# Three 1024x1024 products of a two-layer block, each formed as seven quarter products

## Chip, cores, metric

The kernel runs on one core of one Trainium2 chip. The metric is the device time of one execution in microseconds (us). The program is written out by hand, engine by engine, in one block: TensorE (PE) multiplies, VectorE (DVE) and ScalarE (ACT) move and combine tiles, GpSimd (POOL) helps and issues accumulating transfers, SyncE (SP) issues loads. The engines meet by semaphores only.

## What is computed

Two layers follow one another on x of 512 tokens by 1024 features, all in float32. The part that the change touches ends the mixer of the second layer:

```
mixed  = spatial gating of the first branch      (512 x 1024), in features-by-tokens as u_t
o      = forgetting attention, 16 heads           (512 x 1024), as att_t
merged = sigmoid(gate_b) * (o @ w_branch_b)  +  sigmoid(gate_a) * (mixed @ w_branch_a)
h      = h + merged @ w_out
h      = h + gated feed-forward of rmsnorm(h)     (phases up0, down0, ...)
```

The first layer, ahead of this, is a convolution with a chunked state scan (phases xbc, qk, z, v, wo_ssd, wo_att) and a feed-forward (ff1_g, ff2_g).

## The kernel before

**Precision.** Each float32 operand is split in a high part, rounded to the matmul's own format (ACT copies to `_hi`), and a low part, the rest (DVE subtracts, to `_lo`). A product is three passes: high by high, high by low, low by high (lines 767 to 769).

**Strips.** A weight matrix of 1024x1024 is read in 4 strips of 256 columns, 1 MB each, through three slots (`w_hi`, `w_lo`; the raw strip lies where the slot's low part goes). `strip_split` counts finished strips, `hi_split` high parts. SP loads strip s when the strip three before is used up (`unit_done`, two per strip: line 590). `PHASES` lists all phases with their strips; their order is the order of PE's work.

**A plain phase** (`stream`, `feature_k`) forms 8 output tiles of 128 features x 512 tokens, each over 8 k and 3 passes, in banks 0 to 3 of PSUM. DVE evacuates each tile.

**Seven products, as there is already.** ff2_0 to ff2_2, down0 and down1 take a product of two 2x2 block matrices as seven block products (`seven`, weights made by `A_PARTS`, data by `T_PARTS`). There the data is the stationary operand and 512 weight columns move. The sums of weight parts are formed in SBUF by accumulating transfers that POOL issues (`part_sums`, line 714), each waited for by the next.

**The stage that is changed.** During gate_a DVE evacuates gate tiles, and ACT and DVE split the attention's output (`split_attention`, into b_hi, b_lo). In branch_b DVE multiplies each result tile into `merged`, and low_a splits u_t (into a_hi, a_lo). In branch_a each tile is multiplied into gate_t, added to `merged`, and split into b. In out2 each tile is added to x (`add_x`), and the norm of the next phase (`high`, `square`, `low`, `add_square` under "ffn2") follows tile by tile. `direct_sums`, `direct_rms` form the root (rstd) while PE is in up0. The first evacuations of up0 (`up_pad`) need rstd; up0 uses banks 0 to 3.

**Work that lies early.** In xbc, ACT goes through tiles m: `first_tap(m)`, `silu(m - 1)`, `keep_xs(m - 4)` and every second time the high part of a strip; PE turns tiles with `turn_xs`, after `keep_xs` has freed its bank. Between qk and z, ACT issues on its own DMA queue `cum_kept<-cum` (line 1566), waits for it, and issues `seg_in<-cum_kept` (`load_cum`, line 1575). POOL masks what is loaded (line 647), ACT takes exponentials, DVE multiplies (line 2277), and PE's y matmuls (line 744) wait for that. After the last chunk ACT issues the load of `head_bias` (line 1600), which DVE's memset (line 2338) waits for and the first attention needs. POOL stages that attention's heads right after its share in z.

## Time and profile before

| | us |
|---|---|
| time, median of 3 runs | 1606.91 (1606.77 to 1607.81) |
| time of the profiled execution | 1607.59 |
| its span | 1605.9 |

Busy, of the span: PE 99%, weight loads (PEld) 81%, DVE 67%, ACT 44%, POOL 11%. The transfers move 195 MB at a mean of 122 GB/s, in three queues of weight: q1 (SP's), q0 (POOL's, accumulating), q10 (ACT's).

How to read it: matmuls are pipelined, so the duration of one is longer than its distance from the next; how many start in a stretch gives the pace. "Idle before, releaser" is the time for which an engine stood before an instruction, and what ended that. A row of a transfer issue shows the time that the issuing engine spent, not the transfer.

### The profile page before, as it was taken

To read this page: it belongs to the slowest core of one execution; us is meant where nothing else is said; L and a number is where in the kernel's file an instruction comes from. 1 tells how busy PE (TensorE), PEld (TensorE's weight loads), DVE (VectorE), ACT (ScalarE), POOL (GpSimd) and SP (SyncE) were. 2 spreads that over 40 slices of the span, in tenths; PEclk is the share of its full clock that TensorE was granted. 3 is DMA by queue.
4 is the path that set the end of the run, shared out by engine and by line. 5 is a ranking of instruction groups with operands and counts; after the bars stand their busy time and mean duration, and the time that the engine had idled before them with its cause. 6 is when DMAs were issued, how large, how long until landed. Compare 5 with 4: busy or idle time off the path is not lost.

```text
span 1605.9 us, 20446 instructions
## 1 busy us (share of the span) xinstructions
PE 1587.6 (99%) x8187; PEld 1305.8 (81%) x8187; DVE 1078.5 (67%) x1494; ACT 710.6 (44%) x1018; POOL 181.5 (11%) x263
## 2 busy tenths in 40 slices
PE   9999999999999999999999999999999999999998
PEld 7877777888888888878788887888888888888888
DVE  6756788669393865657744477445566876878857
ACT  6524575545252524415662156342334443443544
POOL 0001055000000000024500255000000000000000
PEclk9999999999999999999999999999999999999999
DMA  5233321264757522331022211322237347344221
GB/s 191 80 106 125 123 95 53 79 210 131 236 132 235 131 106 94 116 138 72 27 105 83 101 53 53 136 101 105 93 143 262 102 135 238 93 154 158 105 106 53
DMA packets 32894, 195.14 MB, mean 122 GB/s; under 512 B 4320, under 2 KB 6816, under 8 KB 11296
## 3 DMA queue, kind: packets, MB, share of 16 engines
q1 hardware_dynamic: 25056, 160.20, 27.0%
q0 software_dynamic: 2880, 20.97, 6.8%
q10 hardware_dynamic: 4864, 12.66, 2.2%
q8 instruction: 65, 1.06, 0.3%
q14 instruction: 29, 0.24, 0.0%
HBM read 187.50 MB, written 6.32 MB: 121 GB/s over the span
## 4 chain that ended last, share of the span: by engine, by line
PE 87%; DVE 7%; issue 2%; ACT 2%; POOL 1%; DMA 0%; DVEq 0%; ACTq 0%; POOLq 0%
PE bank L767 20%; PE bank L769 19%; PE bank L768 19%; PE bank L1189 3%; PE bank L1190 3%; PE bank L1191 3%; PE bank L815 3%; PE bank L817 3%; PE bank L816 3%; PE bank L1000 1%; PE bank L775 1%; PE bank L985 1%; DVE w_lo L2370 1%; PE bank L744 1%; DVE up_c L2668 1%
## 5 line engine op out<-in xcount | busy, mean ns | idle before, releaser
L767 PE MATMUL bank<-a_hi,w_hi 128*128 128x512 f32 x1160 | 456.8, 394 | 0.6 <-DVE x L2030 0.6
L769 PE MATMUL bank<-a_hi,w_lo 128*128 128x512 f32 x1160 | 452.0, 390 | 0.0
L768 PE MATMUL bank<-a_lo,w_hi 128*128 128x512 f32 x1160 | 451.6, 389 | 0.0
L1375 ACT ACTIVATE w_hi<-w_raw 128x2048 fp32r<-128x2048 f32 x95 | 181.3, 1908 | 184.5 <-DMA w_raw<-in_strips 182.7
L769 PEld LDWEIGHTS bank<-a_hi,w_lo 128*128 128x128 f32 x1160 | 217.8, 188 | 45.9
L767 PEld LDWEIGHTS bank<-a_hi,w_hi 128*128 128x128 f32 x1160 | 217.9, 188 | 45.3 <-issue 2.3
L768 PEld LDWEIGHTS bank<-a_lo,w_hi 128*128 128x128 f32 x1160 | 218.0, 188 | 43.0 <-issue 0.2
L1951 DVE TENSOR_TENSOR w_lo<-w_raw,w_hi 128x2048 fp32r<-128x2048 f32 x92 | 210.9, 2293 | 54.4 <-ACT w_hi L1375 54.3
L1189 PE MATMUL bank<-w_hi,t_hi 128*128 128x512 f32 x280 | 109.3, 390 | 0.1
L1191 PE MATMUL bank<-w_hi,t_lo 128*128 128x512 f32 x280 | 109.0, 389 | 0.0
L1190 PE MATMUL bank<-w_lo,t_hi 128*128 128x512 f32 x280 | 109.0, 389 | 0.0
L767 PE MATMUL bank<-b_hi,w_hi 128*128 128x512 f32 x240 | 93.6, 390 | 0.4 <-DVE b_lo L2684 0.4
L768 PE MATMUL bank<-b_lo,w_hi 128*128 128x512 f32 x240 | 93.4, 389 | 0.0
L769 PE MATMUL bank<-b_hi,w_lo 128*128 128x512 f32 x240 | 93.4, 389 | 0.0
L815 PE MATMUL bank<-w_hi,a_hi 128*128 128x512 f32 x224 | 90.8, 405 | 0.0
L714 POOL DMA_DIRECT2D a_part<-in_parts x20 | 17.4, 868 | 643.6 <-DMA a_part<-in_parts 431.9
L816 PE MATMUL bank<-w_lo,a_hi 128*128 128x512 f32 x224 | 87.4, 390 | 0.0
L817 PE MATMUL bank<-w_hi,a_lo 128*128 128x512 f32 x224 | 87.4, 390 | 0.0
L1845 ACT ACTIVATE up_c<-up_pad,conv_w 128x512 f32<-128x512 f32 x44 | 35.8, 816 | 115.1 <-DVE up_pad L2022 115.1
L2668 DVE SCALAR_TENSOR_TENSOR up_c<-up_pad,conv_w,up_c 128x512 f32<-128x512 f32 x88 | 65.8, 747 | 1.8 <-ACT up_c L1845 0.3
L2370 DVE TENSOR_TENSOR w_lo<-a_part,w_hi 128x2048 fp32r<-128x2048 f32 x25 | 57.1, 2285 | 10.7 <-ACT w_hi L1664 10.7
L2022 DVE TENSOR_TENSOR up_pad<-bank,rstd 128x512 f32<-128x512 f32 x44 | 30.3, 691 | 49.4 <-PE bank L769 49.4
(364 smaller groups left out, 2658.0 us busy)
## 6 DMA issues: line engine op xcount, KB each, us to landing
w_raw<-in_strips SPq DMA_DIRECT2D x107, 1024.0 KB, 4.8
a_part<-in_parts SPq DMA_DIRECT2D x25, 1024.0 KB, 7.4
a_part<-in_parts POOLq DMA_DIRECT2D x20, 1024.0 KB, 9.1
spare<-in_parts SPq DMA_DIRECT2D x5, 1024.0 KB, 15.0
spare<-in_strips SPq DMA_DIRECT2D x5, 1024.0 KB, 4.9
seg_in<-cum_kept ACTq DMA_DIRECT2D x16, 256.0 KB, 3.5
x_kept<-x ACTq DMA_DIRECT2D x2, 2048.0 KB, 9.2
x<-x_kept SPq DMA_DIRECT2D x2, 2048.0 KB, 9.9
```

The lines of the kernel that those rows point to most:

```text
L767: mm(ps[:, :], w_hi[slot][:, k, cols], hi[:, k, :], start=(k == 0), stop=False)
L768: mm(ps[:, :], w_hi[slot][:, k, cols], lo[:, k, :], start=False, stop=False)
L769: return mm(ps[:, :], w_lo[slot][:, k, cols], hi[:, k, :], start=False, stop=(k == kt - 1))
L815: mm(bank[j][:, :], hi[:, q, tok], w_hi4[slot][:, k, :], start=(q == 0), stop=False)
L816: mm(bank[j][:, :], hi[:, q, tok], w_lo4[slot][:, k, :], start=False, stop=False)
L817: return mm(bank[j][:, :], lo[:, q, tok], w_hi4[slot][:, k, :], start=False, stop=(q == KT - 1))
L1189: mm(ps[:, :], hi[:, k, tok], w_hi4[slot][:, k, :], start=(first and k == 0), stop=False)
L1190: mm(ps[:, :], hi[:, k, tok], w_lo4[slot][:, k, :], start=False, stop=False)
L1191: last = mm(ps[:, :], lo[:, k, tok], w_hi4[slot][:, k, :], start=False, stop=(end and k == W4 - 1))
L1375: run(w_hi[j], w_raw[j], ACT.Copy).then_inc(hi_split, 1)
L1951: v.tensor_tensor(w_lo[j], w_raw[j], w_hi[j].bitcast(F32), ALU.subtract).then_inc(strip_split, 1)
L2668: v.scalar_tensor_tensor(up_c[q], up_pad[q][:, j:j + T], flat[:, at * (CONV2 + 1) + j:at * (CONV2 + 1) + j + 1], up_c[q], ALU.mult, ALU.ad ...
```

## The change

The phases branch_b, branch_a and out2 get 7 strips each instead of 4: seven products of 512x512 weight parts by 4 k-tiles x 256 tokens. A quarter of the data is a half of the features (k-tiles) by a half of the tokens. The weights are the stationary operand as before, and 256 token columns move. Data sums (four per product) are made on POOL (`fold_sums`), all high parts on ACT and all low parts on DVE. Of the products' results, some are kept and combined on ACT and DVE (`keep_first`, `keep_second`, `keep_sums`, `take`), so that a result quarter is ready after products 3, 5, 6 and 7 (the first by take_first).

The four weight sums that are needed are formed in DRAM (tensor `pre`, 4 kinds x 3 matrices x 1 MB): ACT issues 12 copies DRAM to DRAM in xbc, POOL 6 accumulating transfers ahead of the first attention, 3 behind it and 3 behind the third ff2 phase. SP then loads the 21 strips through two buffers per product (`fold_raw`), in x's place for the first two products, and x itself comes back during out2's start. PE's order of phases and everything from up0 on stay; the strip counts shift by 9.

```diff
+FOLD = ["branch_b", "branch_a", "out2"]
+QUADS = [(0, 0), (1, 0), (0, 1), (1, 1)]
+FOLD_BANK = [4, 6, 4, 6, 2, 6, 2]
+FOLD_QUAD = [0, 1, 2, 0, 1, 3, 2]
+FOLD_SOURCE = [(0, 0), 0, (1, 0), 2, 1, 3, (1, 1)]
+PRE_SUMS = [(0, 1), (0, 0), (0, 0), (1, 0)]
+PHASES += [(name, 7) for name in FOLD]
...
 # SP
+                if s in FOLDED:
+                    n = s - FIRST[FOLD[0]]
+                    if n == 0:
+
+                        sp_eng.wait_ge(pv_done, 2 * 3 * HEADS8)
+                        sp_eng.wait_ge(summed, 16 * (12 + 4 * FF_SEVEN))
+                    elif n == 14:
+
+                        sp_eng.wait_ge(fold_step, FOLD_STEP0 + 5)
+                    elif n == 15:
+
+                        sp_eng.wait_ge(*low_ready(s - 3))
+                    elif n != 1:
+                        sp_eng.wait_ge(*low_ready(s - 2))
+                    f, i = FOLDED[s]
+                    source = FOLD_SOURCE[i]
+                    sp_eng.dma_start(flat(fold_at(s)), fold_part(f, source) if i in (0, 2, 6) else pre[source, f]).then_inc(fold_loaded[n % 3], 16)
+                    if n == 15:
+
+                        sp_eng.wait_ge(*low_ready(s - 2))
+                        sp_eng.dma_start(x, x_kept).then_inc(x_loaded[0], 16)
...
 # POOL
+            pool.wait_ge(copied, 16 * 12)
+            for kind, part in ((0, (1, 1)), (1, (0, 1))):
+                for f in range(3):
+                    pool.dma_start(pre[kind, f], fold_part(f, part), accum_op=ALU.add, max_dma_last_dim=8192).then_inc(summed, 16)
             pool.wait_ge(unit_done, 2 * FIRST["v"] + 2)
             clear_stage1(0)
             attention("1", "qk")
+            pool.wait_ge(summed, 16 * 6)
+            for f in range(3):
+                pool.dma_start(pre[2, f], pre[0, f], accum_op=ALU.add, max_dma_last_dim=8192).then_inc(summed, 16)
...
+            def fold_sums(f, n):
+
+                src, at = fold_src[f], FOLD_SUM0 + 4 * f
+                a11, a12, a21, a22 = (quad(src, *q) for q in ((0, 0), (0, 1), (1, 0), (1, 1)))
+                if n == 0:
+                    if f == 0:
+                        pool.wait_ge(att_out, 3 * HEADS8)
+                    elif f == 1:
+                        pool.wait_ge(a_ready, KT)
+                        pool.wait_ge(unit_done, 2 * FIRST["branch_b"])
+                    else:
+                        pool.wait_ge(merged_ready, 3)
+                    ins = pool.tensor_tensor(quad(fold_three[f], 1, 0), a11, a21, ALU.subtract)
...
 # PE
-            stream("branch_b", feature_k, B, ready=lambda k: pe.wait_ge(att_lo, 4 + k + 1))
-            stream("branch_a", feature_k, A, ready=wait_tiles(amix_lo))
-            stream("out2", feature_k, B, ready=wait_tiles(m_lo))
...
+            def folded(f):
+
+                for i in range(7):
+                    s = FIRST[FOLD[f]] + i
+                    slot, (t, k0) = s % W_SLOTS, QUADS[FOLD_QUAD[i]]
+                    hi, lo = quad(fold_hi[f], t, k0), quad(fold_lo[f], t, k0)
+                    pe.wait_ge(*low_ready(s))
...
+                    for h in range(2):
+                        fold_bank(f, i, h)
+                        for e in range(2):
+                            ps = bank[FOLD_BANK[i] + h][:, e * (T // 2):(e + 1) * (T // 2)]
+                            cols = slice((2 * h + e) * P, (2 * h + e + 1) * P)
+                            for k in range(W4):
+                                mm(ps, w_hi4[slot][:, k, cols], hi[:, k, :], start=(e == 0 and k == 0 and i in (0, 1, 4)), stop=False, skip_group_check=True)
+                                mm(ps, w_hi4[slot][:, k, cols], lo[:, k, :], start=False, stop=False, skip_group_check=True)
+                                last = mm(ps, w_lo4[slot][:, k, cols], hi[:, k, :], start=False, stop=(k == W4 - 1), skip_group_check=True)
+                        last.then_inc(unit_done, 1)
...
 # ACT
+            def copy_parts():
+                for kind, part in enumerate(PRE_SUMS):
+                    for f in range(3):
+                        act.dma_start(pre[kind, f], fold_part(f, part)).then_inc(copied, 16)
...
+                if m == 8:
+                    copy_parts()
...
 # DVE
+            def take(f, i, j, step, at):
+
+                src, e0 = fold_src[f], EVAC0[FOLD[f]]
+                for h in range(2):
+                    product_ready(f, step, h)
...
+                new, gate, total = quad(src, 1, 0), quad(gate3, i, j), quad(merged3, i, j)
+                if f == 0:
+                    fold_do(v.tensor_tensor(total, total, new, ALU.mult))
+                else:
+                    fold_do(v.tensor_tensor(new, new, gate, ALU.mult))
+                    v.tensor_tensor(total, total, new, ALU.add).then_inc(merged_ready, 1)
+                    dve.wait_ge(merged_ready, at // 2)
...
 # DVE's order about the start of out2
+            keep_sums(1)
+            low_strip(1, 5)
+            take_22(1)
+            low_strip(1, 6)
+            low_strip(2, 0)
+            take_21(1)
+            low_strip(2, 1)
+            take_12(1)
+
+            low_four(2, 1)
+            low_four(2, 2)
+            low_four(2, 3)
+            low_strip(2, 2)
+            low_three(2, 0)
             dve.wait_ge(x_loaded[0], 48)
...
+            take_21(2)
+            lo(FIRST["up0"])
+            for m in range(4):
                 low("ffn2", m, gains[:, 5, :], (a_hi, a_lo))
                 add_square("ffn2", m)
+            take_12(2)
+            lo(FIRST["up0"] + 1)
+            for m in range(4, KT):
+                low("ffn2", m, gains[:, 5, :], (a_hi, a_lo))
+                add_square("ffn2", m)
```

## Rows read from the trace of the kernel before

**Rows 1.** The page, part 1: busy time of each engine.

```profile
PE 1587.6 (99%) x8187; PEld 1305.8 (81%) x8187; DVE 1078.5 (67%) x1494; ACT 710.6 (44%) x1018; POOL 181.5 (11%) x263
```

**Rows 2.** Busy time by stretches: length, engines, PE clock, DMA share, GB/s.

```profile
1009.00:1052.50 43.50, 43.50 (x194) 35.98 (x193) 18.64 (x20) 21.40 (x29) 0.00 (x0) 1.00 0.37 145
...
1052.50:1096.10 43.60, 43.60 (x194) 36.12 (x193) 19.04 (x20) 14.08 (x16) 0.00 (x0) 1.00 0.27 97
...
1200.00:1400.00 200.00, 199.94 (x881) 164.93 (x881) 151.94 (x159) 88.10 (x81) 6.04 (x7) 1.00 0.53 169
```

**Rows 3.** DVE in order of time, at up0: start, duration, line, operation.

```profile
1199.37 0.69 DVE L2022 TENSOR_TENSOR up_pad<-bank,rstd 128x512 f32<-128x512 f32 x1
```

**Rows 4.** Groups by form (busy, mean ns), and a stretch with 256-column matmuls.

```profile
L1325 PE MATMUL bank<-a_hi,w_hi 128*128 128x256 f32 x64 | 18.3, 286 | 0.0
...
1575.00:1580.00 5.00, 5.00 (x44) 5.00 (x43) 4.45 (x7) 1.69 (x4) 0.00 (x0) 1.00 0.00 0
```

**Rows 5.** Groups of DVE and ACT: busy us, mean ns of one, idle before.

```profile
L1951 DVE TENSOR_TENSOR w_lo<-w_raw,w_hi 128x2048 fp32r<-128x2048 f32 x92 | 210.9, 2293 | 54.4 <-ACT w_hi L1375 54.3
L2386 DVE TENSOR_TENSOR t_raw<-hid 128x1024 f32<-128x1024 f32 x25 | 30.5, 1218 | 2.2 <-ACT hid L1700 2.1
L1375 ACT ACTIVATE w_hi<-w_raw 128x2048 fp32r<-128x2048 f32 x95 | 181.3, 1908 | 184.5 <-DMA w_raw<-in_strips 182.7
```

**Rows 6.** Groups of POOL by form.

```profile
L674 POOL TENSOR_SCALAR score<-score,row_inv 128x512 f32<-128x512 f32 x8 | 5.6, 695 | 8.8 <-DVE row_inv L2105 8.6
...
L734 POOL TENSOR_TENSOR out_t<-x,rstd 128x256 f32<-128x256 f32 x2 | 1.4, 723 | 188.3 <-ACT rstd L1935 188.3
...
L674 POOL TENSOR_SCALAR score<-score,row_inv x32: 372/588/1210, 221.3 to 294.0; 128x128 f32<-128x128 f32 x8, 128x256 f32<-128x256 f32 x8, 128x384 f32<-128x384 f32 x8, 128x512 f32<-128x512 f32 x8
```

**Rows 7.** POOL and DVE in order of time, where their instructions meet.

```profile
206.14 2.55 POOL L667 TENSOR_SCALAR q_blk<-qk 64x512 fp32r<-64x512 f32 x2
...
205.22 2.29 DVE L1951 TENSOR_TENSOR w_lo<-w_raw,w_hi 128x2048 fp32r<-128x2048 f32 x1 [2.40 <-ACT w_hi L1375]
...
973.41 1.31 POOL L667 TENSOR_SCALAR q_blk<-qk 64x512 fp32r<-64x512 f32 x2
...
974.23 1.57 DVE L1966 TENSOR_TENSOR w_lo<-w_raw,w_hi 128x1024 fp32r<-128x1024 f32 x1
```

**Rows 8.** The page, parts 3 and 6: DMA queues; issues with us to landing.

```profile
q1 hardware_dynamic: 25056, 160.20, 27.0%
q0 software_dynamic: 2880, 20.97, 6.8%
...
w_raw<-in_strips SPq DMA_DIRECT2D x107, 1024.0 KB, 4.8
...
x_kept<-x ACTq DMA_DIRECT2D x2, 2048.0 KB, 9.2
```

**Rows 9.** ACT, DVE and PE in order of time, in xbc and before z.

```profile
67.32 1.91 ACT L1375 ACTIVATE w_hi<-w_raw 128x2048 fp32r<-128x2048 f32 x1
...
74.33 0.81 ACT L1532 ACTIVATE conv<-u_pad,conv_w 128x512 f32<-128x512 f32 x1 [2.56 <-DVE u_pad L2022]
...
119.19 0.33 ACTq L1566 DMA_DIRECT2D cum_kept<-cum  x1
...
120.84 1.31 ACTq L1575 DMA_DIRECT2D seg_in<-cum_kept  x3
...
133.33 2.34 DVE L2277 TENSOR_TENSOR decay<-decay,bank 128x1024 f32<-128x1024 f32 x2
...
135.20 1.10 PE L744 MATMUL bank<-x_dt,decay 128*32 128x64 f32 x64
```

**Rows 10.** The load of head_bias, its landing, and who needs it.

```profile
195.30 0.39 ACTq L1600 DMA_DIRECT2D head_bias<-in_rel  x1
...
DMA to landing us min/median/max: 11.5/11.5/11.5
...
214.00 0.48 DVE L2338 MEMSET head_bias<- 64x512 f32 x1
```

More of the change, by code:

```diff
@@ L1282, in _ @@
+            for f in range(len(FOLD)):
+                folded(f)
             stream("up0", feature_k, A, ready=wait_tiles(NORMS["ffn2"]["lo"]), after=lambda j: direct_sums("ffn2") if j == 0 else None)
@@ L1784, in _, with sigmoids @@
             attention("2b", "gate_b", None)
-            def sigmoids(phase, where):
-                for j in range(KT):
+            def sigmoids(phase, where, first, last):
+                for j in range(first, last):
                     act.wait_ge(dve_evac, EVAC0[phase] + j + 1)
@@ L1808, in _, with high_strip @@
-            for i in range(2, 4):
-                hi(FIRST["branch_b"] + i + 2)
-            for m in range(KT):
-                act.wait_ge(merged_ready, m + 1)
-                if m == 0:
-                    act.wait_ge(unit_done, 2 * FIRST["branch_a"])
-                run(b_hi[:, m, :], merged[:, m * T:(m + 1) * T], ACT.Copy).then_inc(m_hi, 1)
-                if m % 2 == 0:
-                    hi(FIRST["branch_a"] + m // 2 + 2)
-            for m in range(KT):
-                act.wait_ge(dve_evac, EVAC0["out2"] + m + 1)
+            def high_strip(f, i):
+                s = FIRST[FOLD[f]] + i
+                act.wait_ge(fold_loaded[(s - FIRST[FOLD[0]]) % 3], fold_count(s))
+                act.wait_ge(unit_done, 2 * (s - W_SLOTS) + 2)
+                run(w_hi[s % W_SLOTS], fold_at(s), ACT.Copy).then_inc(hi_split, 1)
@@ new lines, in keep_second @@
+            def keep_second(f):
+                if f:
+                    act.wait_ge(dve_evac, EVAC0[FOLD[f - 1]] + 10)
+                for h in range(2):
+                    act.wait_ge(unit_done, 2 * FIRST[FOLD[f]] + 2 + h + 1)
+                    run(fold_q[h], halves(6 + h), ACT.Copy).then_inc(snapped, 1)
+            sigmoids("gate_b", merged, 0, KT)
+            hi(FIRST["gate_a"] + 2)
+            high_four(0, 0)
+            high_four(0, 1)
+            hi(FIRST["gate_a"] + 3)
+            high_four(0, 2)
@@ L2641, in _ @@
-            dve.wait_ge(x_loaded[0], 48)
-            for m in range(KT):
-                add_x("out2", m, m)
+                if 1 <= j <= 4:
+                    low_four(0, j - 1)
+                if j in (4, 6):
+                    low_strip(0, j // 2 - 2)
+            low_four(1, 0)
+            low_strip(0, 2)
+            low_three(0, 0)
+            low_four(1, 1)
+            low_strip(0, 3)
+            low_three(0, 1)
+            low_strip(0, 4)
+            take_first(0)
+            low_four(1, 2)
@@ new lines, in _ @@
+            low_three(0, 2)
+            keep_sums(0)
+            low_strip(0, 5)
+            low_four(1, 3)
+            take_22(0)
+            low_strip(0, 6)
+            low_strip(1, 0)
+            take_21(0)
+            low_strip(1, 1)
+            take_12(0)
+            low_strip(1, 2)
+            low_three(1, 0)
+            low_strip(1, 3)
+            low_three(1, 1)
+            low_strip(1, 4)
+            take_first(1)
+            low_three(1, 2)
+            low_four(2, 0)
```

315 lines of the change are left out of this document (254 added, 61 removed).

## Prediction

> **What bounds the kernel now.** I read the header of the page first: TensorE (PE) is busy 1587.6 us of a span of 1605.9 us and its granted clock is full in every stretch I asked for [rows 2], so time is lost or won only where matmuls disappear or where PE comes to stand still [rows 1]. Then the table by stretches over the four stages that the change touches. In gate_a, branch_b, branch_a and out2 PE is busy all of the 43.5 us of each; VectorE (DVE) works 19 to 24 us in each, ScalarE (ACT) 12 to 21 us, GpSimd (POOL) not at all (two of the four rows stand in [rows 2]). So the three products to be changed cost 3 x 43.6 = 130.8 us, all of it PE time, and the other engines have room. No wait of PE falls into them, nor into the start of up0 behind them; the first evacuation there comes at 1199.37, when the root of the norm is ready [rows 3].
>
> **What a product costs on PE.** A 1024x1024x512 product is 8 output tiles x 8 k x 3 passes = 192 matmuls of 512 columns, 43.6 / 192 = 0.227 us each. Seven quarter products of 2 halves x 2 x 4 k x 3 = 48 matmuls of 256 columns are 336. The trace has such matmuls at the end of the kernel (L1325, each with a weight load of its own): 44 in 5 us, 0.1136 us each, with the weight-load row full at 5.00 of 5 us [rows 4]. Their mean of 286 ns is a latency, as 390 ns is for the wide ones. So a product costs 336 x 0.1136 = 38.2 us, and three save 3 x (43.6 - 38.2) = **16.3 us**, if PE never waits. The weight loads leave no room for a narrower matmul, but at 256 columns the pace is exactly half of that at 512, so I take nothing off for them.
>
> **What DVE must do for it.** Durations: 2.29 us for a strip's low part, 1.22 for 128x1024, 0.69 for 128x512 [rows 3, 5]. Each product has 7 strips (16.0) and 7 quarter low parts of the data (8.5) = 24.5. To that branch_b adds 2 first takes, 4 operations of keep_sums and 3 x (2 takes and a 1.22 multiply): 1.4 + 2.8 + 7.8, in all 36.5 us. Branch_a has four more 1.22 additions, 41.4 us. Out2 has three known parts (3.8) and no multiplies: 36.7 us. Back-to-back operations overlap by 0.09, so some 3 us come off each. Against 38.2 us of PE, DVE thus goes from half busy to full, and only what it does ahead in gate_a (four low parts and two strips, 9 us, where it is idle 25 us [rows 2]) gives slack. ACT has 7 x 1.91 + 7 x 1.06 + 4 x 0.6 = 23 us, which is no bound.
>
> **What POOL does to DVE.** Each product adds 4 subtractions or additions of 128x1024 with two inputs on POOL. The trace has none of that size. One-input rows go from 0.37 us (128 columns) to 0.695 (512), the only two-input one is 0.723 us for 256 columns [rows 6]. Bounds: 0.27 fixed + 4 x 0.46 = 2.1 us, and 4 x 0.723 = 2.9 us. I take 2.1, since the one-input rows show the fixed part. The Trainium skill (GPSIMD Engine Reference, section Elementwise) gives 4497 ns for 2048 elements, so an estimate by it would be about 2.3.
> More important is who waits. At 206.14 a POOL pair of copies takes 2.55 us (1.32 otherwise) while DVE runs a strip's low part until 207.51. At 974.23 a DVE low part of 128x1024 takes 1.57 us for 1.22, while POOL's pair of copies runs until 974.72 [rows 7]. Both engines stand until the other's instruction is over, when DVE reads two SBUF inputs. DVE operations that read a bank beside one SBUF input (the takes) never grow there. So eight POOL operations in branch_a and out2 can each hold DVE for up to 2.1 us, and be held for up to 2.3.
>
> **Where PE waits then.** I laid the three products out, in each engine's program order, with these durations. PE starts branch_b at 1052.5. In branch_b the waits are 0.6 and 0.2 us, on strips 5 and 6; in branch_a 0.2. The strip cycle carries it narrowly: two buffers, each 4.8 (load) + 1.9 (ACT) + 2.3 (DVE) = 9.0 us of the 10.9 that two products last [rows 5, 8].
> The costly place is the start of out2. Its second product needs the difference of two merged quarters, of which one comes from branch_a's sixth product. From that product's end PE has two products of work, 10.9 us. DVE has, in order: the rest of a strip (1.8), two takes, a multiply and an addition (3.7), a strip (2.2), the seventh product's two takes, multiply and addition (3.8), and only then the low part of the difference (1.1): 12.6 us. POOL's subtractions lie in between and hold the last multiply, the addition and the low part for 0.7, 1.9 and 2.0: 17.2 us. PE waits 17.2 - 10.9 = **6.2 us**, and 0.8 more one product later; without the holding 1.7 us.
> In out2 there is 0.4 more (strip 6). At up0 the fifth norm tile waits for the last take (1.1 us), and the column sums, which need all eight tiles, 0.5 us. Sum: 0.8 + 0.2 + 6.2 + 0.8 + 0.4 + 1.6 = 10.0, and 0.1 for each of seven restarts of PE: 10.7. Late gain: 16.3 - 10.7 = **5.6 us**.
> With POOL at 2.9 us the gain is 0.5; with no holding it is 12; with loads of 6 us instead of 4.8 (x comes back, 2 MB, in the same queue) 0.6, and with both 3 us are lost. The root chain behind out2 has cover: before, rstd is ready at 1199.37, while PE, in up0 since 1183, needs its fifth bank only at 1205 (four units of 5.44) [rows 3]; 5 us late costs nothing. After up0 nothing changes, and DVE at 152 of 200 us [rows 2] keeps what was won.
>
> **The early part: DMA.** Copies. At 69.2, behind the high part that begins at 67.32, ACT issues 12 transfers of 1 MB, DRAM to DRAM. Issuing three takes 1.31 us, so twelve hold ACT for 5.2 us, to 74.4. Behind them stand first_tap(9), silu(8) and keep_xs(5), and PE's turn_xs(7), which needs the last of these some 3.4 us into its twelfth unit; ACT idles 2.56 us just before 74.33, and one tile lasts 5.4 us, so it has caught up a tile later [rows 9]. Cost 0, or 0.5 if an issue takes longer.
> The queue itself: on ACT's queue, 1 MB each, in order, then comes cum_kept at 119.19 and the seg_in loads, at 120.84, whose chain (DVE 133.33) ends in PE's matmuls at 135.20 [rows 9]. Slack in it is 4.5 us (DVE is busy until 133.3 with other work). The price of a copy isn't in the trace. Bounds: the strip queue moves 160.20 MB in 27.0% of 1605.9 us, 2.8 us per MB transfer; the accumulating one 20.97 MB in 6.8%, 5.5 us [rows 8]. With strips beside (14 us) the copies are through at 69.5 + 34 + 11 = 115, or at 69.5 + 66 + 17 = 152. PE waits max(0, end - 123.7): 0 to 28 us, from 3.4 us per copy on. I take the lower end, as each byte still passes an engine once, and stores keep up with loads (2 MB in 9.2 us, by the row of x_kept [rows 8]), but this is the weakest step.
> The Trainium skill (DMA: Bandwidth & Descriptors, section Latency and other measured facts) speaks against that: copies between HBM tensors at 207 to 214 GB/s per direction. By it a copy takes 4.9 us and PE would wait 22 us; no run here shows it yet.
> Accumulations. POOL issues 6 at 183, when its share of the decays is done; behind them stands the staging of attention 1. They last 6 x 5.5 = 33 us, or half more as both sides are DRAM. Beside them head_bias (issued 195.3, landed 206.8) is needed by DVE at 214.0 [rows 10]: 7.2 us of slack. With its 5.7 us of transfer and every third turn it lands at 212, cost 0. The later six lie beside matmul stages with no short deadline; cost 0.
>
> **Sum.** The profiled execution took 1607.6 us (span 1605.9, 1.7 around it), the median of the three is 1606.9, 0.7 less. 1607.6 - 5.6 = 1602.0, and beside the median **1601.3 us**.
>
> **The rivals.** (1) The copies stand before seg_in and z stops: slower. It decides from 3.4 us per copy, and outweighs the 5.6 from 3.9 on. At 4.2, halfway between the rows, it costs 11 (1612), at 5.5 it costs 28 (1629). For it: one queue, in order, and a chain with 4.5 us of slack. Against it: the full rate of stores. Chance 0.27. By the page's rate it would be 1623. (2) The accumulations crowd head_bias out until they are through (232): 18 late, 7.2 covered, 11 us, 1612. Chance 0.11. (3) POOL's and DVE's operations don't hold each other when long: gain 12, 1595. Chance 0.10. (4) The two-buffer strip cycle falls behind (loads of 6 us, POOL at 2.9): 3 us lost, 1610. Chance 0.10. That it doesn't shorten PE's work at all (256-column matmuls bound by weight loads) has against it the 44 in 5 us; under 0.01.
>
> **How the numbers follow.** Forecast 0.42, with a range of its own from 1597 to 1605. A measurement tells some 0.2% (3.2 us) from no change. Faster: 0.38 of the forecast and (3), 0.48. Same: 0.04 of the forecast, 0.07 of (4), 0.03 of (2) and (1), 0.14. Slower: most of (1) and (2), 0.03 of (4), 0.38. The range goes from 1595 to 1622: it leaves out the dear half of (1) and the low end of (3).
>
> **What would show it.** PE's rows in the folded products at 0.1136 us a piece and 38.2 us a product; a wait of PE of about 6 us some 5 us into out2, ended by DVE's low_four; POOL rows of 2.1 us, or 3 to 4 beside DVE's; DVE rows of a strip over 4 us beside them; seg_in landing near 124 and z starting as before. If PE waits near 135 on the decay chain with seg_in landing at 135 or later, rival (1) has it; if near 215 to 230 behind the DVE memset of head_bias, (2). The prediction is wrong, with all else right, if copies between DRAM tensors cost over 3.9 us each.

## The result, and the profile after

| | before | after |
|---|---|---|
| median of four runs, us | 1607.12 | 1642.24 (1641.65 to 1642.85) |
| ratio | | 1.0218 (95% interval 1.0200 to 1.0236) |
| span of the profiled execution, us | 1605.9 | 1641.1 |

The changed kernel is 35.1 us slower, where 5.6 us less had been predicted (1601.3). The header of its page, to be laid beside [rows 1]: PE's busy time has hardly grown, the span has by 35 us, so PE stands.

```profile
PE 1591.2 (97%) x8619; PEld 1327.8 (81%) x8619; DVE 1135.9 (69%) x1518; ACT 741.2 (45%) x1036; POOL 227.5 (14%) x287
```

I compared the start of the same matmuls in both traces. How much later than before they start: 0 us until 87 us; 9.3 after xbc; 13.4 at the end of z; 27.4 in attention 1; 34.8 at ff1_0, and still 34.8 where branch_b starts (1087.27 for 1052.5). The three changed products take 129.7 us (1087.27 to 1217.0) where they took 130.5, so up0 starts 34.0 late. There PE stands 0.8 us for the fifth norm tile (`a_lo`, at 1223.4), and from then on it is 35.1 to 35.2 to the end. The whole loss thus lies hundreds of microseconds ahead of the products. The products gain 0.8 us, and up0 takes that back.

**The early losses.** ACT in order of time, then PE, in xbc of the changed kernel (start, duration, engine, line, operation; in brackets the idle time before it and what ended it):

```profile
67.52 6.43 ACTq L1549 DMA_DIRECT2D pre<-in_parts  x10
74.06 0.82 ACT L1693 ACTIVATE conv<-u_pad,conv_w 128x512 f32<-128x512 f32 x1 [4.94 <-issue]
...
89.98 1.91 ACT L1535 ACTIVATE w_hi<-w_raw 128x2048 fp32r<-128x2048 f32 x1 [11.60 <-DMA w_raw<-in_strips]
...
93.75 1.09 PE L1155 MATMUL bank<-ident,bc_t 128*128 128x128 f32 x4 [6.47 <-ACT xs_tok L1683]
```

The strip that ACT waits for was issued at 67.51, together with the twelve copies. It lands 22.4 us later; in the kernel before, it took 5.5. ACT goes through its list in order, so the tiles behind that high part are late too, and PE with them. What moved in the two queues from 66 to 90 us (packets, MB, share of the time of the engines):

```profile
q10 hardware_dynamic: 208, 7.34, 84.3%
q1 hardware_dynamic: 160, 1.18, 14.8%
```

Without the packets of 4 bytes these are 112 packets of 64 KB for ACT's copies and 144 of 8 KB for SP's strips: the two queues moved about as many packets, and the copies six times the bytes. The next place is attention 1, by DVE and PE in order of time:

```profile
238.96 0.48 DVE L2582 MEMSET head_bias<- 64x512 f32 x1 [11.97 <-DMA head_bias<-in_rel]
...
240.13 0.45 PE L1091 MATMUL bank<-k_blk,q_blk 128*128 128x128 f32 x1 [11.79 <-DVE vs L2319]
```

The list of transfer issues (count, size, median us from issue to landing) has the reason:

```profile
pre<-in_parts POOLq DMA_DIRECT2D x6, 1024.0 KB, 26.0
...
head_bias<-in_rel ACTq DMA_DIRECT2D x1, 2048.0 KB, 32.9
```

head_bias landed after 11.5 us before [rows 10]. The third place is ff1_0, where PE stands 4.9 us for DVE's x. Ahead of it a strip issued at 327.53, behind the three accumulating transfers of 322.38, landed after 11.8 us for 4.8. Stretches of 5 us at the three places, in the columns of [rows 2]:

```profile
90.00:95.00 5.00, 1.25 (x5) 1.25 (x6) 3.04 (x3) 3.60 (x4) 0.00 (x0) 0.76 0.82 269
95.00:100.00 5.00, 5.00 (x14) 3.89 (x13) 2.02 (x3) 2.09 (x4) 0.00 (x0) 0.55 1.19 446
...
235.00:240.00 5.00, 0.00 (x0) 0.00 (x0) 1.04 (x3) 0.00 (x0) 0.00 (x0) 0.50 0.52 199
240.00:245.00 5.00, 4.87 (x13) 3.94 (x14) 4.13 (x8) 0.00 (x0) 0.00 (x0) 0.50 0.02 3
...
355.00:360.00 5.00, 3.27 (x8) 2.65 (x9) 3.42 (x6) 3.50 (x5) 0.51 (x1) 0.55 1.01 426
```

Behind each long stand the granted clock is 0.50 to 0.55, the 1.2 GHz level, for some 5 us after PE has work again: each stand costs 2 to 3 us more than its own length.

**The late stage.** The stretches of the three products, from the first matmul of each to the first of the next, and two of 5 us inside the last:

```profile
1087.27:1127.58 40.31, 40.31 (x337) 40.31 (x336) 34.34 (x26) 23.78 (x21) 12.40 (x4) 1.00 0.46 167
1127.58:1168.03 40.45, 40.45 (x339) 40.38 (x337) 35.56 (x29) 19.70 (x16) 0.00 (x0) 1.00 0.57 209
1168.03:1217.00 48.97, 42.52 (x338) 42.34 (x337) 45.70 (x37) 23.68 (x24) 14.18 (x4) 0.93 0.44 157
...
1175.00:1180.00 5.00, 0.00 (x0) 0.00 (x0) 4.97 (x2) 2.96 (x3) 4.14 (x2) 0.81 0.01 5
1180.00:1185.00 5.00, 4.60 (x22) 4.63 (x23) 5.00 (x4) 3.24 (x5) 3.24 (x1) 0.51 0.00 0
```

Two products run without a stand and take 40.3 and 40.5 us, not 38.2: 336 matmuls, 0.120 us from start to start. The expectations below were written with 39.8 us and 0.1185 us; those came from stretches that end four matmuls short of the product, so read 40.3 and 0.120 for them. In out2 PE stands for 6.5 us before 1180.4 while DVE is busy without a break, then runs at 0.51.

### The profile page after: what moved, and what is told of

Read it like the earlier page. It is cut to its first block, busy times and chain, and to the rows that moved or that the text cites. A ratio compares the mean times of both kernels' runs of the same rounds, so it can differ in the third digit from the quotient of the medians.

```text
span 1641.1 us, 21457 instructions
## 1 busy us (share of the span) xinstructions
PE 1591.2 (97%) x8619; PEld 1327.8 (81%) x8619; DVE 1135.9 (69%) x1518; ACT 741.2 (45%) x1036; POOL 227.5 (14%) x287
## 3 DMA queue, kind: packets, MB, share of 16 engines
q0 software_dynamic: 4608, 33.56, 10.5%
## 4 chain that ended last, share of the span: by engine, by line
PE 81%; DVE 7%; DMA 6%; issue 3%; ACT 2%; POOL 1%; DVEq 0%; ACTq 0%; POOLq 0%
PE bank L887 16%; PE bank L888 16%; PE bank L889 16%; PE bank L1309 3%; PE bank L1310 3%; PE bank L1311 3%; DMA w_raw<-in_strips 3%; PE bank L935 2%; PE bank L1433 2%; PE bank L1434 2%; PE bank L1435 2%; PE bank L937 2%; PE bank L936 2%; DMA head_bias<-in_rel 2%; PE bank L1120 1%
## 5 line engine op out<-in xcount | busy, mean ns | idle before, releaser
L887 PE MATMUL bank<-a_hi,w_hi 128*128 128x512 f32 x1096 | 434.4, 396 | 5.6 <-DVE x L2278 4.9
L889 PE MATMUL bank<-a_hi,w_lo 128*128 128x512 f32 x1096 | 429.0, 391 | 0.0
L888 PE MATMUL bank<-a_lo,w_hi 128*128 128x512 f32 x1096 | 428.9, 391 | 0.0
L889 PEld LDWEIGHTS bank<-a_hi,w_lo 128*128 128x128 f32 x1096 | 206.9, 189 | 43.9
L1535 ACT ACTIVATE w_hi<-w_raw 128x2048 fp32r<-128x2048 f32 x83 | 158.4, 1909 | 185.5 <-DMA w_raw<-in_strips 183.7
L888 PEld LDWEIGHTS bank<-a_lo,w_hi 128*128 128x128 f32 x1096 | 207.3, 189 | 40.6 <-issue 0.2
L2199 DVE TENSOR_TENSOR w_lo<-w_raw,w_hi 128x2048 fp32r<-128x2048 f32 x80 | 183.4, 2293 | 76.8 <-ACT w_hi L1535 76.6
L1433 PE MATMUL bank<-b_hi,w_hi 128*128 128x256 f32 x224 | 64.5, 288 | 6.5 <-issue 6.5
L2614 DVE TENSOR_TENSOR w_lo<-a_part,w_hi 128x2048 fp32r<-128x2048 f32 x25 | 57.1, 2285 | 10.7 <-ACT w_hi L1827 10.7
L1434 PE MATMUL bank<-b_lo,w_hi 128*128 128x256 f32 x224 | 64.3, 287 | 0.0
L1435 PE MATMUL bank<-b_hi,w_lo 128*128 128x256 f32 x224 | 64.3, 287 | 0.0
```

The source lines that it names most:

```text
L887: mm(ps[:, :], w_hi[slot][:, k, cols], hi[:, k, :], start=(k == 0), stop=False)
L888: mm(ps[:, :], w_hi[slot][:, k, cols], lo[:, k, :], start=False, stop=False)
L889: return mm(ps[:, :], w_lo[slot][:, k, cols], hi[:, k, :], start=False, stop=(k == kt - 1))
L1433: mm(ps, w_hi4[slot][:, k, cols], hi[:, k, :], start=(e == 0 and k == 0 and i in (0, 1, 4)), stop=False, skip_group_check=True)
L1535: run(w_hi[j], w_raw[j], ACT.Copy).then_inc(hi_split, 1)
L2199: v.tensor_tensor(w_lo[j], w_raw[j], w_hi[j].bitcast(F32), ALU.subtract).then_inc(strip_split, 1)
```

## The experiments

All ratios are to the kernel before, run beside each of them on the same chip (its medians are 1606.92 to 1607.49 us).

| run | median us | ratio, 95% interval |
|---|---|---|
| e1_no_sums | 1607.87 | 1.0005 (0.9995 to 1.0014) |
| e2_copies | 1616.86 | 1.0061 (1.0046 to 1.0076) |
| e3_moved | 1612.78 | 1.0033 (1.0022 to 1.0045) |
| e4_difference | 1608.96 | 1.0013 (1.0003 to 1.0022) |
| e5_quiet | 1607.98 | 1.0002 (0.9993 to 1.0011) |
| e6_order | 1604.25 | 0.9980 (0.9971 to 0.9989) |
| e7_early_sums | 1644.14 | 1.0228 (1.0214 to 1.0242) |
| e8_one_by_one | 1653.92 | 1.0289 (1.0275 to 1.0303) |
| e9_halves | 1614.72 | 1.0047 (1.0034 to 1.0060) |
| e10_packets | 1640.70 | 1.0212 (1.0196 to 1.0227) |
| e11_three | 1607.89 | 1.0003 (0.9994 to 1.0012) |
| e12_before_strip | 1616.09 | 1.0052 (1.0035 to 1.0069) |

### Which part of the loss belongs to what: e1 and e2

e1 takes out `copy_parts`, the three groups of accumulating transfers and the waits on them:

```diff
-                if m == 8:
-                    copy_parts()
...
-                    sp_eng.dma_start(flat(fold_at(s)), fold_part(f, source) if i in (0, 2, 6) else pre[source, f]).then_inc(fold_loaded[n % 3], 16)
+                    sp_eng.dma_start(flat(fold_at(s)), fold_part(f, source if i in (0, 2, 6) else (0, 1))).then_inc(fold_loaded[n % 3], 16)
```

> The changed kernel without its twelve copies and without its twelve accumulating transfers; the four kinds of sum strips are loaded from plain weight parts of the same size, so the weight sums are left out of the computation. Only the three folded products differ from the kernel before. Theory A (the 34.8 us by which the changed kernel is late when branch_b starts all come from the DRAM traffic of the sums; the three products take 129.7 us for 130.5 before): 1606.3 us, 0.8 less than before, PE standing 7 us at the second product of out2 as in the changed kernel, and no loss before branch_b. Theory B (the products themselves, through POOL and DVE in attention and split work, cost part of it): 1610 us or more. Pace of the 256-column matmuls: 0.1185 us, 39.8 us for a product without a wait.

Measured 1607.87: theory A, 1.6 us above its number. The early waits are gone, and the wait of 6.5 us in out2 is there. So the three products as they are bring nothing that can be told from zero. The pace in the expectation doesn't hold: the first two products take 40.3 and 40.5 us here as well.

e2 puts the twelve copies back, at their place.

> The changed kernel with its twelve copies where they are and without the twelve accumulating transfers (the weight sums are left out of the computation, strips are loaded from the copies). Theory A (copies alone make the strip of xbc late, accumulations make head_bias and the strips of ff1_0 late): the shift of 9.3 us at 105 us stays and nothing is added until branch_b; 1606.3 + 9.3 = 1615.6 us, landing of head_bias back near 11.5 us. Theory B (the later losses are after-effects of the copies or of the shift): 1625 us or more.

Measured 1616.86, 9.0 us more than e1, with PE standing 7.6 us for xs_tok in xbc and head_bias landing after 10.2 us: theory A. The rest of the loss of the changed kernel, 1642.2 - 1616.9 = 25.3 us, comes with the accumulating transfers.

### The same bytes elsewhere: e3 and e5

e3 keeps all the work and moves it: copies behind the strips 4 to 15, now on SP's own queue, all accumulations behind the third ff2 phase. Of its edit, the copies:

```diff
+                if 4 <= s < 4 + 12:
+                    kind, f = divmod(s - 4, 3)
+                    sp_eng.dma_start(pre[kind, f], fold_part(f, PRE_SUMS[kind])).then_inc(copied, 16)
```

> The changed kernel, computing everything, with the DRAM traffic moved: SP issues one copy behind each of the strips 4 to 15 instead of ACT twelve at once, and POOL issues all twelve accumulating transfers behind the third ff2 phase, where the DMA share of the kernel before is 0.2 to 0.4 for 100 us. Theory A (it is the crowding of a strip or table with a deadline that costs, not the bytes): strips land in about 10 us, their slack is about 17 us, no loss before branch_b; 1606.3 us, the same as without any sums. Theory B (DRAM to DRAM traffic slows strips whenever it runs): over 1612 us, with waits of PE behind strips in xbc or ff1_3.

Measured 1612.78, its executions spread from 1609.98 to 1613.54, and neither theory's number. The profiled one (1610.49) shows one new wait, 3.2 us of PE for DVE's decay in z, the chain of seg_in; where the slower executions lose up to 3 us more wasn't seen. In xbc no strip was late: each was issued ahead of its copy, in the same queue, and the one at 67.28 landed after 6.1 us. e5 avoids z too, with four copies behind each of the strips 19, 20 and 21, in attention 1.

> The changed kernel, computing everything, with all traffic of the sums in quiet stretches: SP issues four copies behind each of the strips 19, 20 and 21 (in attention 1, where the DMA share of the kernel before is 0.12 and a strip is wanted every 25 us), POOL issues the twelve accumulating transfers behind the third ff2 phase. The run with moved traffic still lost 3.2 us in z, where DVE waited for decay: two of its copies shared the engines with seg_in there. Theory A (only a load with a deadline beside the traffic costs time): no wait for decay, no other new wait before branch_b, 1607.9 us, as without any sums. Rival (copies or accumulations cost wherever they lie): 1611 us or more.

Measured 1607.98, as e1 without any of the traffic: 24 MB of transfers are free where nothing with a deadline waits behind them. Place is only part of that: e3 and e5 also took the copies out of ACT's queue and put them behind the strips in the strips' own, and by e3 they cost nothing in xbc either that way. Copies on ACT's queue in smaller packets weren't tried. The stretches with the first four copies and one strip, 5 MB in 15 us (the last lands at 257.0), while PE works on:

```profile
241.00:246.00 5.00, 5.00 (x31) 4.03 (x30) 4.52 (x13) 2.50 (x9) 2.13 (x3) 1.00 1.08 419
246.00:251.00 5.00, 5.00 (x29) 4.23 (x28) 4.70 (x9) 1.80 (x5) 3.43 (x6) 1.00 1.15 421
251.00:256.00 5.00, 4.50 (x29) 3.61 (x28) 3.80 (x12) 3.92 (x8) 1.22 (x3) 1.00 0.64 210
```

### The accumulations ahead of attention 1: e7, e8, e10

e7 spreads the copies as e3 does and leaves the accumulations where the change has them.

> The changed kernel, computing everything, with its accumulating transfers where they are (six at 183 us ahead of attention 1, three behind it, three behind the third ff2 phase) and only the copies spread, one behind each of the strips 4 to 15. The run with both moved took 1612.8. Theory A (the six accumulations crowd out head_bias, which lands at 32.9 us instead of 11.5, and the next three make strips of ff1_0 late: together 25 us): 1607.9 + 3 to 5 (decay) + 23 to 26 = 1634 to 1638 us. Theory B (in the changed kernel the two groups of traffic only cost that much together, the second starting from an already late and cold stretch): 1620 to 1628 us.

Measured 1644.14: above theory A's range, not below it. The last copy now lands at 197, and POOL waits for it, so that the six are issued at 197.36, some 3 us ahead of head_bias instead of some 14. head_bias lands after 40.3 us, and PE stands 19.6 us. The nearer the crowd is to the load with the deadline, the dearer: the accumulations cost 25 us in the changed kernel; they and the spread copies, with the 3.2 us of decay, cost 36 us here. In both runs head_bias lands only when the last of the six has: at 238.8 behind 236.4 in the changed kernel, at 240.9 behind 239.5 here.

e8 lets each of the six wait for the one before.

> As the run with spread copies and early accumulations, but each of the six accumulations ahead of attention 1 waits for the one before it, so that one at a time shares the engines with other loads. POOL then stands behind them until about 183 + 6 x 9 = 237 us before it stages attention 1. Theory A (what costs is how many transfers are under way when head_bias is issued): head_bias lands in 12 to 20 us, but POOL's staging of attention 1, some 10 us before that behind the transfers, is now late instead and PE waits for k_blk or q_blk: 1630 us or more. Theory B (the share of the engines counts, not the number): head_bias lands as late as with six, about 33 us, and the time is that of the other run.

Measured 1653.92. One accumulation alone lands after 7.7 us, and head_bias after 20.6, so one transfer beside it takes less from it than six do. But POOL comes to its staging of attention 1 at 244.6 and PE stands 31.8 us. That is theory A: waiting between transfers only moves the loss from the DMA engines to POOL's queue.

e10 changes the changed kernel in one number. It had been meant to give rows of 2 KB. It gives packets of 512 bytes: the page counts 16128 packets for 33.56 MB in q0, where the changed kernel has 4608, and that is sixteen for each packet of 8 KB in the six transfers.

```diff
-                    pool.dma_start(pre[kind, f], fold_part(f, part), accum_op=ALU.add, max_dma_last_dim=8192).then_inc(summed, 16)
+                    pool.dma_start(pre[kind, f], fold_part(f, part), accum_op=ALU.add, max_dma_last_dim=512).then_inc(summed, 16)
```

> The changed kernel, computing everything, with one edit: the six accumulating transfers ahead of attention 1 are split in rows of 2 KB, the size that head_bias has, instead of 8 KB. Theory A (the queues take turns by packet, so a queue with packets four times as long gets four times the bytes, and head_bias waits for them): head_bias lands in 15 to 20 us instead of 32.9, the wait of 11.8 us at attention 1 nearly goes, 1628 to 1632 us. Theory B (the turns go by bytes, or small accumulating packets cost so much more that the transfers last longer): head_bias lands at 33 us or later, 1642 us or more.

Measured 1640.70. head_bias lands after 16.1 us for 32.9, as theory A has it. What moved beside it, POOL's q0 and ACT's q10, in the changed kernel (206 to 236 us) and in e10 (203 to 219):

```profile
q0 software_dynamic: 609, 4.34, 71.3%
q10 hardware_dynamic: 726, 1.49, 13.6%
...
q0 software_dynamic: 2039, 1.04, 51.0%
q10 hardware_dynamic: 1040, 2.10, 38.5%
```

But the time doesn't follow, for a reason that neither theory had. POOL in e10:

```profile
190.46 5.74 POOL L778 DMA_DIRECT2D pre<-in_parts  x3
225.96 5.51 POOL L778 DMA_DIRECT2D pre<-in_parts  x3 [29.77 <-issue]
231.51 0.52 POOL L772 MEMSET k_blk<- 64x512 f32 x1
```

With sixteen times as many packets POOL comes to a stand between its third and fourth issue for 29.8 us. Its queue being full is my reading; the row says only that it waited for nothing that the profile shows. The fourth issue starts at 225.96, and the third transfer had landed at 225.71. The staging of attention 1 (q_blk, k_blk) is then late, and PE stands 16.9 us.

The stand also muddies the comparison: while head_bias was under way only three of the six had been issued. That fewer transfers alone do it is against e8, where head_bias took 20.6 us beside one at a time in packets of 8 KB, longer than beside two or three in small ones. So the size of the packets matters; how much of the 16.8 us between 32.9 and 16.1 it explains isn't shown.

### Three transfers and one strip: e11 and e12

e11 is e5 with three of the twelve accumulations back behind attention 1.

> As the run with all traffic in quiet stretches, except that three of the twelve accumulating transfers (pre of kind 2 from kind 0) are issued right behind attention 1, where the changed kernel has them; they come ahead of the ones that fill their source, so the weight sums are not the right ones. Theory A (beside the strips and the weight parts of ff1_0 these three, 1.0 of the DMA share from 325 to 345 us in the changed kernel, make a strip late and PE stands 4.9 us, with a clock of 0.55 behind it): 1608.0 + 6 to 7.6 = 1614 to 1616 us. Theory B (the wait at ff1_0 was an after-effect of the lateness of attention 1): 1608 to 1610 us.

Measured 1607.89: nothing lost, by its number theory B. Before taking that for the answer I looked at the order of issue: POOL had waited for the last copy, and issued the three at 301.63, 1.5 us behind the strip of 300.13, which landed after its usual 4.8 us. In the changed kernel the three come at 322.38 and the strip at 327.53. e12 restores that order by ending the copies one strip earlier:

```diff
-                if s in (19, 20, 21):
-                    for c in range(4 * (19, 20, 21).index(s), 4 * (19, 20, 21).index(s) + 4):
+                if s in (19, 20):
+                    for c in range(6 * (19, 20).index(s), 6 * (19, 20).index(s) + 6):
```

> As the run with three accumulating transfers behind attention 1, except that the twelve copies go six behind strip 19 and six behind strip 20, so that POOL no longer waits for the last of them and issues the three some 5 us before the strip of wo_att instead of 1.5 us behind it. In that run the strip was issued at 300.13, the three at 301.63, and nothing was lost; in the changed kernel the three were issued at 322.38, the strip at 327.53, which landed after 11.8 us for 4.8. The weight sums are again not the right ones. Theory A (the order of issue decides: a strip with no slack that is issued behind the three waits for its share): landing near 12 us, ACT waits 7 us for it, PE stands 4 to 5 us and has a clock near 0.55 behind it, 1613 to 1616 us. Theory B (the wait at ff1_0 in the changed kernel was an after-effect of the late attention 1): 1608 us.

Measured 1616.09. POOL issues at 294.95, SP the strip at 300.06, and it lands after 12.4 us. ACT and PE in e12, and after them the stretch behind the stand:

```profile
312.48 1.92 ACT L1538 ACTIVATE w_hi<-w_raw 128x2048 fp32r<-128x2048 f32 x1 [7.83 <-DMA w_raw<-in_strips]
...
329.88 0.77 PE L890 MATMUL bank<-a_hi,w_hi 128*128 128x512 f32 x1 [4.85 <-DVE x L2279]
```

```profile
330.00:335.00 5.00, 5.00 (x12) 3.98 (x13) 3.60 (x6) 3.84 (x5) 0.87 (x1) 0.50 1.07 367
```

Theory A: 8.2 us between e11 and e12 (8.6 when each is set against the kernel before beside it) for the same three transfers, issued 5 us ahead of a strip without slack or 1.5 us behind it. This is the changed kernel's loss at ff1_0, and it would be there without the other two.

### The pace of a narrow matmul: e9

The products took 40.3 to 40.5 us without a wait. To see whether that belongs to the width or to the folded form, e9 narrows the plain products of the kernel before:

```diff
+            def halves_k(ps, slot, u, act, k, kt=KT):
...
+                for w, data in ((w_hi, hi), (w_hi, lo), (w_lo, hi)):
+                    for h in range(2):
+                        half = slice(T // 2 * h, T // 2 * (h + 1))
+                        last = mm(ps[:, half], w[slot][:, k, cols], data[:, k, half], start=(k == 0 and h == 0 and w is w_hi and data is hi),
...
-            stream("branch_b", feature_k, B, ready=lambda k: pe.wait_ge(att_lo, 4 + k + 1))
...
+            stream("branch_b", halves_k, B, ready=lambda k: pe.wait_ge(att_lo, 4 + k + 1))
```

> The kernel before, computing everything, with one edit: in its plain branch_b, branch_a and out2 every matmul of 512 token columns becomes two of 256, with the same weights and the same number of columns in all (192 x 2 = 384 per product for 192). Nothing else moves. Theory A (a matmul has a fixed part of about 0.010 us beside its columns, as 0.2267 us at 512 and 0.1185 us at 256 columns show): 3 x (384 x 0.1185 - 43.6) = 3 x 1.9 = 5.7 us more than before, 1613.0 us, 45.5 us for each of the three products. Theory B (the pace is proportional to the columns, as the prediction had it, and the 0.1185 of the folded products has another cause, such as their banks or the read of data quarters): 1607.3 us, no change.

Measured 1614.72, 7.4 us more than the 1607.31 beside it: theory A. The three products take 138.2 us (1052.07 to 1190.30), 0.120 us a matmul, the same as the folded ones; with that pace theory A's sum is 3 x (384 x 0.120 - 43.5) = 7.7 us. No wait of PE is new. The same number of columns in twice as many matmuls costs 6% of a product (46.1 us for 43.5). Every matmul here has a weight load of its own, so the number of both doubles; whether the fixed part belongs to the matmul or to the load isn't shown.

### The start of out2: e4 and e6

e4 is e1 with the first difference on DVE:

```diff
-            fold_sums(2, 0)
+            pool.wait_ge(fold_sum, FOLD_SUM0 + 9)
...
             take_21(1)
+            v.tensor_tensor(quad(fold_three[2], 1, 0), quad(merged3, 0, 0), quad(merged3, 1, 0), ALU.subtract).then_inc(fold_sum, 1)
             low_strip(2, 1)
+            low_four(2, 1)
             take_12(1)
-            low_four(2, 1)
```

> As the run without sums (weight sums left out), with one edit in out2's start: the first difference of merged quarters is formed on DVE right behind the third quarter's addition instead of on POOL, and its low part comes ahead of the last quarter's four operations. Theory A (PE stands 7.0 us there because DVE's queue is too long and POOL and DVE hold each other, and loses 2.3 us more at the granted clock of 0.51 behind it): the low part is ready near 1173 on the changed kernel's scale, the stand shrinks to 0 to 1.5 us, and the kernel takes 1606.3 - 7.8 = 1598.5 us. Rival: the last quarter comes late instead and PE waits for the third product by as much; 1603 to 1606 us.

Measured 1608.96, no gain: the rival, and stronger than it was put. The second product starts 1.0 us late instead of 6.5, and the third then waits 6.5 us for its strip's low part, which starts on DVE at 1148.03 behind the last quarter's work and takes 4.0 us there for 2.3. The granted clock falls again (0.56). The list of waits showed only the wait that came last; behind it, everything on DVE and ACT was as late.

e6 is e5 with the order changed throughout: two sums of merged quarters on DVE, strip 2 and the snapshot of the first product (now into gate_t) ahead of the last quarter's low parts.

```diff
             take_21(1)
+            v.tensor_tensor(quad(fold_three[2], 1, 0), quad(merged3, 0, 0), quad(merged3, 1, 0), ALU.subtract).then_inc(fold_sum, 1)
             low_strip(2, 1)
+            low_four(2, 1)
+            v.tensor_tensor(quad(merged3, 1, 0), quad(merged3, 1, 0), quad(merged3, 1, 1), ALU.subtract).then_inc(fold_sum, 1)
             take_12(1)
...
-            low_four(2, 1)
+            low_strip(2, 2)
...
 # ACT
             high_four(2, 1)
+            high_strip(2, 2)
+            keep_first(2)
             high_four(2, 2)
```

> As the run with all traffic in quiet stretches, and with the start of out2 rearranged: the first two sums of merged quarters are formed on DVE (the first right behind the third quarter's addition), the snapshot of out2's first product goes to the free quarter of gate_t instead of one that must first be split, and the low part of the difference and strip 2 come ahead of the low parts that the last quarter needs. The earlier run that moved only the difference ended its first wait and got one of 6.5 us for the third product's strip, since that strip and the snapshot stood behind the last quarter on DVE and ACT. Theory A (DVE's queue sets the sum of the waits, but short waits don't lower the granted clock): waits of about 2.7 and 2.1 us at the third and fourth product for 7.0 at the second, and no stretch at a clock of 0.51, so 2.2 + 2.3 = 4.5 us less than the run in quiet stretches, 1603.4 us. Rival (a wait of the same sum appears elsewhere, as in the earlier run): 1607 to 1609 us.

Measured 1604.25, 3.7 us less than e5 and 0.2% less than the kernel before (3.2 us; interval 1.8 to 4.7). It is the only version that beats it. (One of its eleven executions took 9038.95 us; its cause isn't known, and it isn't in this comparison.) The three products take 125.9 us instead of the 129.3 of e5. Three things were changed together, so which of them did it isn't shown. PE in e6 waits 2.5 us once and 0.6 one product later, and the clock falls for a moment only:

```profile
1145.00:1150.00 5.00, 2.65 (x13) 2.68 (x14) 5.00 (x4) 5.00 (x6) 2.61 (x1) 0.76 0.53 198
1150.00:1155.00 5.00, 4.82 (x37) 4.61 (x35) 4.96 (x3) 2.48 (x3) 0.62 (x1) 0.90 0.04 15
```

## Why the prediction was wrong

**"A product costs 38.2 us": wrong, 40.3.** The step that failed is reading "44 in 5 us" [rows 4] as a pace. A stretch counts the matmuls that touch it, those in flight at its edge included: of the 44, 41 start in it. The distance stood in the trace of the kernel before, in the same matmuls:

```profile
1575.71 0.28 PE L1325 MATMUL bank<-a_hi,w_hi 128*128 128x256 f32 x1
...
1576.08 0.28 PE L1325 MATMUL bank<-a_hi,w_hi 128*128 128x256 f32 x1
...
1576.43 0.28 PE L1325 MATMUL bank<-a_hi,w_hi 128*128 128x256 f32 x1
```

These are every third matmul, six distances in 0.72 us: 0.120 us. At 512 columns it is 0.2267, so a matmul, with its weight load, costs 2 x 0.120 - 0.2267 = 0.013 us beside its columns, not a share of them. The gain at full pace is 3 x (43.5 - 40.3) = 9.6 us, not 16.3; e9 shows the same cost without the folding. The Trainium skill (TensorE: Matmul & The Clock Gate, section Wait — 56ns, not 53.3ns?) gives columns over 2.4 GHz and 2.5 ns: by that estimate it would be 0.109 us. The trace of these matmuls, each with a weight load of its own, disagrees.

**The wait at the start of out2: right.** 6.2 and 0.8 us had been forecast, at the second and third product; 6.5 came, at the second. The rows show why as it was put: POOL and DVE hold each other.

```profile
1168.12 4.52 POOL L822 TENSOR_TENSOR fold_three<-merged 128x1024 f32<-128x1024 f32 x1 [56.59 <-DVE merged L2937]
1172.71 3.21 POOL L825 TENSOR_TENSOR merged<-merged 128x1024 f32<-128x1024 f32 x1
...
1173.76 3.25 DVE L2937 TENSOR_TENSOR merged<-merged,u_t 128x1024 f32<-128x1024 f32 x1
1177.04 3.25 DVE L2868 TENSOR_TENSOR b_lo<-fold_three,b_hi 128x1024 fp32r<-128x1024 f32 x1
```

The addition and the low part had been given 1.9 and 2.0 us for being held; they take 3.25 us each for 1.22. When DVE doesn't hold it, such a POOL operation takes 2.40 us (at 1087.58 and 1090.06), between my 2.1 and the bound of 2.9. The Trainium skill's figure (GPSIMD Engine Reference, section Elementwise), an estimate of 2.3, was nearer. What the sum left out is the clock: 22 matmuls instead of some 38 start in the 4.6 us behind the stand, 2 us more.

**Late gain 5.6 us: wrong, nothing.** From the start of branch_b to the end the changed kernel is 0.4 us slower (34.8 us late, then 35.2), and e1, 0.8 us above the kernel before, can't be told from no change. The mis-sized term is the pace: 9.6 us for 16.3. The losses came near their sum, 10.0 us for 10.7: 8.8 in the three products, 2 of them from the clock, and 1.2 at up0 for 1.6.

**Copies, cost 0: wrong, 9 us.** The price of a copy was right: the twelve, with their strips, take from 66.3 to 111.8 us, and 34 + 11 us had been worked out. seg_in wasn't late by itself (3.4 us to landing), so rival (1) fell. What failed is a step that was never costed: a strip beside the copies was counted for what it does to their end, not for what they do to its landing. Before, that strip landed at 73.1 and ACT took it up at 77.58, 4.5 us of slack; now it landed 17 us later. Its packets of 8 KB ran beside packets of 64 KB, and the size of a packet doesn't occur in the prediction. The Trainium skill's 207 to 214 GB/s for copies between HBM tensors (DMA: Bandwidth & Descriptors, section Latency and other measured facts), stated for tiles with a pitch between their rows, doesn't hold for these; the transfers of e5 moved 419 and 421 GB/s, the second figure with copies alone under way.

**Accumulations ahead of attention 1, "lands at 212, cost 0": wrong.** The mechanism was rival (2), with a chance of 0.11: head_bias landed only when all six were through, at 238.8, after 32.9 us. PE stood 11.8. The rival's price had a slip in it: through at 232 and needed at 214.0 is 18 us, with the slack already used, and 7.2 us were taken off once more to give 11. Starts went from 9.3 to 27.4 us late, 18.1, but that the numbers agree is partly chance. Of it 4.1 came at the end of z, where a strip issued at 193.78 beside the same transfers landed after 12.0 us for 4.8, and some 3 from the clock behind the stand at attention 1. In the forecast head_bias got "every third turn", as if turns had the same size. From 206 to 236 us it moved 1.49 MB in packets of 2 KB while the accumulations moved 4.34 MB in packets of 8 KB; with packets of 512 bytes beside it (e10) it lands in half the time. The Trainium skill (DMA: Bandwidth & Descriptors, section Queues, rings and completion order) says that the engines take turns between queues packet by packet; e10 agrees, and head_bias, in rows of 2 KB, is on the bad side of that.

**"The later six lie beside matmul stages with no short deadline; cost 0": half wrong.** The three at 586 cost nothing. The three behind attention 1 cost some 7 us in the changed kernel and 8.2 in e12, through one strip without slack.

**The direction** thus hung on three loads with deadlines, all passed over or priced at zero, while the argument dwelt on the one chain that turned out safe. Their cost is 35 us. Without them (e1, e5) the kernel is still not faster: there it is the pace that had been taken too fast, and the clock.

## What to carry to other kernels

Before bytes are put in an "idle" stretch, list every load that is issued while they are under way, with its slack and the size of its packets, and as a first bound let each land late by the whole of the traffic under way (head_bias did; the strip of 67.51 by 17 of 45 us). Average DMA share says nothing about it: twelve copies on a second queue, in a stretch with a share of 0.2 to 0.3, cost 9 us through the strip of 67.51, and the same copies cost nothing there when each followed a strip in the strip's own queue (e3). Take a pace from the distance of starts, never from a count in a stretch, and take a product's time from its first matmul to the next product's first; a product cut in narrower matmuls pays a fixed part for each. And where one engine is full over several products, taking out one late operation only shows the next: count its whole queue up to the second and third deadline before moving anything.

## What was not expected of the hardware

- Issuing a copy from DRAM to DRAM takes ACT about 0.61 us (and SP mostly 0.49 to 0.6, in e3 and e5), a strip load takes SP 0.33.
- POOL can stand for 29.8 us in the middle of issuing transfers, with transfers in packets of 512 bytes under way (e10). Issues of an accumulating queue aren't a fixed cost of about 0.9 us.
- The copies and a strip moved 419 and 421 GB/s over 5 us (e5); the accumulating transfers and what ran beside them, from 195 to 235 us of the changed kernel with a full share, only 230 to 290.
- Copies between DRAM tensors went in packets of 64 KB, strips in 8 KB, head_bias in 2 KB, and beside each other the queues moved packets at rates much nearer to one another than their bytes (112 to 144 in xbc, for 7.3 and 1.2 MB).
- A stand of 2.5 us (e6) let the clock dip to 0.76 and 0.90 in the stretches around it; those of 4.9 to 12 us were followed by 0.50 to 0.56.
